# Where the rotary multiplications of queries and keys run: GpSimd or VectorE

## The reference, cut to what matters

```python
def rope_1d(x, pos):
    half = x.shape[-1] // 2
    ...
    x1, x2 = x[..., :half], x[..., half:]
    return jnp.concatenate([x1 * cos - x2 * sin, x2 * cos + x1 * sin], axis=-1)

def rope_2d(x, rows, cols):
    h = x.shape[-1] // 2
    return jnp.concatenate([rope_1d(x[..., :h], rows), rope_1d(x[..., h:], cols)], axis=-1)
```

## Time and profile before

| | |
|---|---|
| median of 3 runs | 2328.52 us (2326.39 to 2328.91) |
| the profiled execution | 2325.39 us, of it the span 2323.7 us |
| PE busy | 2249.2 us, 97% |
| DVE busy | 1336.8 us, 58% |
| ACT busy | 937.2 us, 40% |
| POOL busy | 154.6 us, 7% |
| input stage of layer 0 / of layer 1 | about 60 to 250 us / 1400 to 1550 us of the span |

### The profile page before, as it was taken

The page is one execution under the profiler, slowest core; times in us unless marked ns, Lnnn a source line. Parts: engine busy times, 40 slices in busy tenths (PEclk is TensorE's granted clock), DMA queues, the critical chain, the costliest instruction groups (busy, mean ns, idle before and its releaser), DMA issues.

```text
span 2323.7 us, 35196 instructions
## 1 busy us (share of the span) xinstructions
PE 2249.2 (97%) x12956; PEld 1878.4 (81%) x12956; DVE 1336.8 (58%) x1958; ACT 937.2 (40%) x1387; POOL 154.6 (7%) x165
## 2 busy tenths in 40 slices
PE   6999988999999999999999999999999999999999
PEld 4789666888888878888888877777788887888887
DVE  7555576566667465435534566656755566545555
ACT  4554666422323343213312346556643334424332
POOL 0113010000000000000000002210100000000000
PEclk8999999999999999999999999999999999999999
DMA  7111010344434211111111131111055552222223
GB/s 290 55 64 64 28 41 20 109 155 134 138 138 164 77 64 63 64 63 64 63 60 61 62 129 64 67 61 59 11 172 173 170 186 77 99 94 97 96 94 118
DMA packets 58786, 221.26 MB, mean 95 GB/s; under 512 B 6753, under 2 KB 6753, under 8 KB 57905
## 3 DMA queue, kind: packets, MB, share of 16 engines
q1 hardware_dynamic: 44496, 160.46, 20.2%
q0 software_dynamic: 14176, 59.26, 7.4%
HBM read 214.45 MB, written 5.24 MB: 95 GB/s over the span
## 4 chain that ended last, share of the span: by engine, by line
PE 88%; DVE 6%; ACT 3%; issue 2%; DMA 1%; SPq 0%; DVEq 0%; ACTq 0%
PE PS L631 85%; PE PS L959 2%; DVE TM L1562 1%; ACT W_hi L1136 1%; DVE SM L1831 1%; ACT XY L1136 1%; DMA FA<-w_mod 1%; DVE W_lo L1559 1%; DVE F_lo L1559 1%; ACT TM L1136 1%; DVE H_lo L1562 0%; DVE XY L1562 0%; ACT F_hi L1136 0%; DVE PS L1842 0%; DVE XY L1865 0%
## 5 line engine op out<-in xcount | busy, mean ns | idle before, releaser
L631 PE MATMUL PS<-H_hi,W_hi 128*128 128x512 f32 (+1 forms) x2256 | 805.6, 357 | 16.0 <-DVE H_lo L1562 5.7
L631 PE MATMUL PS<-H_lo,W_hi 128*128 128x512 f32 (+1 forms) x2256 | 793.9, 352 | 0.0
L631 PE MATMUL PS<-H_hi,W_lo 128*128 128x512 f32 (+1 forms) x2256 | 792.9, 351 | 0.0
L1559 DVE TENSOR_TENSOR W_lo<-W_st,W_hi 128x1024 fp32r<-128x1024 f32 x278 | 342.4, 1232 | 553.8 <-ACT W_hi L1136 552.5
L1136 ACT ACTIVATE W_hi<-W_st 128x1024 fp32r<-128x1024 f32 x278 | 293.7, 1057 | 827.5 <-PE PS L631 822.8
L631 PEld LDWEIGHTS PS<-H_hi,W_hi 128*128 128x128 f32 x2256 | 427.1, 189 | 88.9 <-issue 22.0
L631 PEld LDWEIGHTS PS<-H_lo,W_hi 128*128 128x128 f32 x2256 | 427.3, 189 | 58.6 <-issue 2.6
L631 PEld LDWEIGHTS PS<-H_hi,W_lo 128*128 128x128 f32 x2256 | 426.9, 189 | 57.9
L631 PE MATMUL PS<-F_hi,W_hi 128*128 128x512 f32 (+1 forms) x968 | 343.1, 354 | 9.7 <-DVE XY L1562 3.1
L631 PE MATMUL PS<-F_lo,W_hi 128*128 128x512 f32 (+1 forms) x968 | 340.5, 352 | 0.0
L631 PE MATMUL PS<-F_hi,W_lo 128*128 128x512 f32 (+1 forms) x968 | 339.6, 351 | 0.0
(11 more groups left out here) (131 smaller groups left out, 2006.5 us busy)
## 6 DMA issues: line engine op xcount, KB each, us to landing
W_st<-w_all SPq DMA_DIRECT2D x278, 512.0 KB, 3.5
RA<-w_mod POOLq DMA_DIRECT2D x40, 512.0 KB, 3.7
TM<-w_mod POOLq DMA_DIRECT2D x40, 512.0 KB, 3.7
FA<-w_ada SPq DMA_DIRECT2D x8, 512.0 KB, 15.7
XY<-bias_na POOLq DMA_DIRECT2D x2, 1792.0 KB, 8.1
XY<-x_in SPq DMA_DIRECT2D x4, 768.0 KB, 12.1
x_spill<-XY POOLq DMA_DIRECT2D x1, 3072.0 KB, 10.5
RA<-w_mod SPq DMA_DIRECT2D x5, 512.0 KB, 9.7
```

Of the source, the lines that this page charges most:

```text
L631: return nc.tensor.matmul(o, lhsT, rhs, start=start, stop=stop)
L1559: return nc.vector.tensor_tensor(o, a, b, f)
```

## The change

The three instructions of each rotation leave POOL's queue, with its wait for the tables, and are put on DVE's queue directly behind the shuffle. DVE waits for the shuffle before the first product and for the two products before the addition. Operands, shapes and the signals that others wait for are the same. POOL's addition of the mask (L607) is not touched.

```diff
@@ on POOL
-            done_rope = [0]
-
-            def rotate(l):
-
-                tt = nc.gpsimd.tensor_tensor
-                for it in items(l):
-                    if it.rope is None:
-                        continue
-                    n = 3 * done_rope[0]
-                    done_rope[0] += 1
-                    pool.wait_ge(S["rope_shuf"], done_rope[0])
-                    dl, s = rope_operands(it)
-                    r0, r1 = (64, 96) if it.rope else it.rows
-                    tt(s, s, ROPE[r0:r1, it.rope + 1, :], ALU.mult).then_inc(S["rope_step"], 1)
-                    tt(dl, dl, ROPE[r0:r1, it.rope, :], ALU.mult).then_inc(S["rope_step"], 1)
-                    pool.wait_ge(S["rope_step"], n + 2)
-                    tt(dl, dl, s, ALU.add).then_inc(S["rope_step"], 1)
-
@@
                 begin(pool, p0 + PH_NORM1 + 1, "act", "dve")
-                pool.wait_ge(S["rope_loaded"], 16)
-                rotate(l)
-
                 pool.wait_ge(S["sg_lo"], 2 * (l + 1))
@@ on DVE, in in_stage
                         wait(dve, "rope_step", base["rope_step"] + 3 * n_rope)
                         nc.vector.stream_shuffle(s, dl, ROT_MLA if it.rope else ROT_GQA).then_inc(S["rope_shuf"], 1)
+                        o0, o1 = (64, 96) if it.rope else it.rows
+                        dve.wait_ge(S["rope_loaded"], 16)
+                        dve.wait_ge(S["rope_shuf"], base["rope_shuf"] + n_rope + 1)
+                        tt(s, s, ROPE[o0:o1, it.rope + 1, :], ALU.mult).then_inc(S["rope_step"], 1)
+                        tt(dl, dl, ROPE[o0:o1, it.rope, :], ALU.mult).then_inc(S["rope_step"], 1)
+                        dve.wait_ge(S["rope_step"], base["rope_step"] + 3 * n_rope + 2)
+                        tt(dl, dl, s, ALU.add).then_inc(S["rope_step"], 1)
                         n_rope += 1
```

## The result

The changed kernel took 2330.17 us (median of 18 runs, 2325.83 to 2331.67), the kernel before on the same chip 2325.71 us (18 runs, 2322.93 to 2329.93). The ratio is 1.0017, with a 95% interval of 1.0011 to 1.0023: +4.0 us, between +2.6 and +5.3. +4.0 us is within 0.2%, and the upper end of the interval reaches over it. The forecast was +3.6 us. One launch of all, among those of the run with layer 1 alone, took 4465.40 us and is left out of its ratio.

A forecast was written before the change was run, and what follows sets the result against it. PE, busy 97% of the span, was taken to bound the kernel. Delays at four places, 0.8 + 1.7 + 0.45 + 0.65 = 3.6 us, added to the 2328.5 us median gave 2332.1 us; range 2327.3 to 2337.0.

The forecast's parts named there:

- kr: Layer 1, kr, gk and gq0: the split behind kr's shuffle comes late, so PE's block starts 0.8 us later.
- mq0 and mq1: Layer 1: mq1's newton and the split come late, delaying PE's statistic 0.8 us and its block 1.7 us in all.
- mq2 in layer 1: The split and last newton move back, so PE's transposes start at 1523.8 instead of 1523.35: +0.45 us.
- in layer 0: Layer 0, mq2: split and newton move back, delaying PE's transposes at 209.21 us by 0.65 us.
- The signs: Right if PE's waits grow at the places named; wrong if elsewhere, rotation outside 1.8 to 2.6 us, or loss made up.
- The price of a rotation: Added DVE time from shuffle to next instruction: 2.2 us for kr and mq, about 2.1 with overlap; bounds 1.8 to 2.6.
- The prediction's 2.71: Time in us from shuffle's start to next instruction's start with overlap, as for 128 rows: 0.78 + 0.60 + 0.73 + 0.60.
- for 32 rows I take no overlap for the three new ones either: New DVE instructions of 32 rows taken without overlap, from the shuffle's 0.75 us: 2.93 us in place of 0.75.
- rival 1: Slower because a rotation on DVE costs more; at the 2.6 us bound +6.4 us, 2334.9 us; chance 0.27.
- slope of 7: With d more per rotation, PE's losses grow by 3d, 2d, d and d: 3.6 + 7d us.
- Rival 2: No cost because POOL's lock on DVE was the larger part: +0.8 us, 2329.3 us; chance 0.17.
- rival 3: Faster, as DVE's waits for POOL and PE's other input-stage waits end: 2325.4 us at best; chance 0.05.

The follow-up runs named there:

- layer 1 alone: Changed kernel with only layer 1's eight rotations on DVE, layer 0's kept on GpSimd: 2329.05 us against 2325.39 of the kernel before, ratio 1.0018.
- layer 0 alone: Changed kernel with only layer 0's eight rotations on DVE, layer 1's kept on GpSimd: 2325.97 us, ratio 1.0001 to the kernel before.
- before's second: The kernel before, unchanged, run again for a second profile: 2326.00 us, ratio 0.9999; profiled span 2323.8 us.

## Why the prediction was right

- **The bound and the place.** It was right to look for waits of PE rather than for DVE's busy time. The change in the trace is four waits at the four places named, 3.1 us against 3.6: kr 0.73 (0.8 predicted), mq0 and mq1 1.62 (1.7), mq2 in layer 1 0.35 (0.45), in layer 0 0.42 (0.65). The measured +4.0 us (2.6 to 5.3) holds both sums. That the runs with layer 1 and with layer 0 alone come to +4.2 and +0.2, and that deferring the same instructions takes it all back, shows the cause; it is not only argued. Profiles with the same start agree: layer 1 alone is 2.5 us over before's second, where its three places have 2.7. The signs were met less exactly: PE's wait rows grew to 3.6 us in layer 1 where 4.5 were predicted, and to 1.9 in layer 0 where 2.2 were.
- **What was luck.** That the total came as near as 0.4 us. The four places give 3.1, of which some 0.6 us are regained at 291 and 1664 us, where the prediction let nothing be regained and named that as a sign of being wrong. The 2.5 left lie just under the interval. The stretch of low clock, which was not in the sum, would add 1.4 us where it occurs; in both profiles of the changed kernel it does.
- **The price of a rotation.** Predicted 2.2 us for 32 rows and 2.1 for 128; measured (1432.66 - 1429.81) - 0.75 = 2.10 for kr, and 2.13 for gk (1439.73 - 1436.97 in place of 0.63). The prediction's 2.71 for rows with overlap gives 2.1 only against that 0.63; against its own 0.75 it is 1.96. The step "for 32 rows I take no overlap for the three new ones either" was wrong. The second product starts 0.61 us after the first (1430.63 to 1431.24), as with 128 rows. What I had read as a property of 32 rows, the 0.75 us from kr's shuffle to the split, is one of the change of place: the shuffle writes partitions 64 to 95 and the split starts at partition 0. The addition shows it: behind kr's, in the same partitions, the split starts after 0.71 us; behind gk's, of all 128 rows, after 0.61 us (1439.12 to 1439.73). The Trainium skill ("VectorE: DVE Perf Modes", section "Two Vector instructions with no wait between them") says just this: an instruction whose operands start in another group of 32 partitions than those before is held until they have ended. All of these starts agree. The prediction cited the section on the drain instead, by which the second product could not start after 0.61 us.
- **The relief of the port.** Predicted DVE busy 1365 us, measured 1353.6. The prediction's own terms, 1336.8 + 33 - 10, make 1360. The additions are as sized, 48 x 0.68 = 33 us; groups by form of the changed kernel (count, busy us, mean ns):
```profile
L1538 DVE TENSOR_TENSOR TM<-TM,ROPE 32x512 f32<-32x512 f32 x10 | 6.8, 683 | 1.0
L1538 DVE TENSOR_TENSOR FA<-FA,ROPE 32x512 f32<-32x512 f32 x10 | 6.8, 676 | 0.0
...
L1538 DVE TENSOR_TENSOR TM<-TM,ROPE 128x512 f32<-128x512 f32 x6 | 4.2, 693 | 0.6
```
  So 33 - 16.8 = 16 us came back from instructions that POOL had stretched, where I took 10, a number that I had not worked out from rows. Near 87 us the split takes 1.23 us again in place of 2.13, near 117 us 1.22. It gave PE nothing, because those instructions were not the ones PE waited for, except for up to 0.5 us in layer 1 by the run without rotations.
- **The rivals.** A dearer rotation (rival 1) falls with the 2.10 us; its slope of 7 holds for small d and steepens beyond. Rival 2, no cost because the lock was larger, had the larger lock (16 us) and still falls: a relief in busy time is not one in waits. A gain (rival 3) was limited to 3.1 us, the waits of the two stages; the run without any rotation gained 2.8 by the medians, 0.5 of it in those waits.
- **The median.** The forecast of 2332.1 us starts from 2328.52, the median of three runs. Over 18 runs that kernel's median is 2325.71, so the predicted time is 1.9 us high though the step was 0.4 us low. The runs of before lie in three groups, near 2323.4, 2325.8 and 2328.9 us, and those of the changed kernel near 2326.2, 2328.8 and 2331.3. Three runs of one kernel place it to some 3 us. The long or short stretch of low clock at the start, worth 2.0 us, later stretches of 1.1 to 1.6 us and the start order at the mask, 1.6 us, are of the size of these steps. The granted clock fits: of the 102 runs of before beside the experiments, the 15 at 0.998 have a median of 2323.4 us, the 11 at 0.995 one of 2329.0. Which of the three a launch without a profile had, no record shows.

## What to carry to other kernels

Work moved to an engine that is 40% idle cost nothing here by its amount and 3 to 4 us by its place in the queue: look at what stands behind the insertion, and who waits for that. The rotations were needed much later, the weight split behind them at once; issued behind the splits, they cost nothing. Judge engines that share ports by who waits for the stretched instruction, not by the sum of the stretching.

## What the runs showed of the hardware

- A start order of 0.1 us between POOL and DVE decides over 1.9 us of one DVE instruction, and 1.6 us of PE's waits. One kernel's profiles show both sides, so a second profile of the same kernel is needed before such a difference is put down to a change.
- On DVE, the second of two instructions of 512 elements starts 0.60 to 0.61 us after the first with no wait between them, 0.71 to 0.72 with a wait or with a change of the group of partitions, and 0.82 us behind a shuffle that it waits for; 32 rows cost what 128 do.
- PE was granted 1.2 instead of 2.4 GHz for 10.1 us of the stretch from 28 to 50 us in nine of the fourteen profiles and for 13.6 us or more in five, the same kernel having both; this moves all that follows by some 2 us.
- Later stretches of about 3.4 us at 1.2 GHz come in ten of the fourteen profiles, near 264 us in three of them, with the same busy share of PE ahead of it (13.50 to 13.56 of 16 us) as in before's first profile (13.50), which does not have the stretch. One near 264 us costs 1.4 us, one at 1957 us nothing.
